# Turning a modulation group one step behind its products in a fused two-layer inference kernel

## The reference

```python
def adaln_params(cvec, w_mod, b_mod):              # once per layer, for c_ctx and for c
    m = jax.nn.silu(cvec) @ w_mod + b_mod          # (1024) @ (1024, 6 * 1024)
    ...                                            # -> sh1, sc1, g1, sh2, sc2, g2

def latent_layer(x, mods, ...):
    sh1, sc1, g1, sh2, sc2, g2 = mods
    h = rmsnorm(x, ln1_g) * (1 + sc1) + sh1
    (cb, cc, ch), (nq, nk, nv), (mq, mk, mv), mo, ig, fg = project(h, w_in, ml_gate_b)
    conv_o = cb * short_conv(cc * ch, conv_w)
    na_o = neighbourhood_attention(nq, nk, nv, k_ctx, v_ctx, na_rpb)
    ml_h, _, _, _ = mlstm_bidir(axial_rope(mq), axial_rope(mk), mv, ig, fg, C0, n0, m0)
    ml_o = mlstm_readout(ml_h, mo, ml_norm_g)
    x = x + g1 * merge(conv_o, na_o, ml_o, w_out)
    h2 = rmsnorm(x, ln2_g) * (1 + sc2) + sh2
    x = x + g2 * hier_moe(h2, ...)                 # 16 experts, top-2 in the top-1 group
    return x
```

## Time and profile before

| | us |
|---|---|
| median of 3 executions (1231.61 to 1316.1) | 1233.97 |
| the profiled execution, its own time | 1231.81 |
| its span | 1230.0 |
| PE busy in the span | 1145.1 |
| DVE busy | 409.4 |
| ACT busy | 250.2 |
| mean granted clock of PE, as a share of full speed | 0.975 |

### The profile page before, as it was taken

How to read it: one execution, slowest core, us unless ns; L and a number is a source line. 1 busy time by engine, 2 the same in 40 slices (tenths; PEclk the granted TensorE clock), 3 DMA queues, 4 the chain that set the end, 5 groups by cost and what they waited for, 6 DMA issues and landing times.

```text
span 1230.0 us, 15289 instructions
## 1 busy us (share of the span) xinstructions
PE 1145.1 (93%) x6240; PEld 623.2 (51%) x6240; DVE 409.4 (33%) x1150; ACT 250.2 (20%) x515; POOL 56.5 (5%) x82
## 2 busy tenths in 40 slices
PE   3999999898989999999989999998998999999996
PEld 3546555576544533554434564566654554355333
DVE  4402041355270333223252302224727032322234
ACT  2210121152132010110142011214413201011013
POOL 1230000000002000000020000000000000000001
PEclk8999999999999999999999999999998999999998
DMA  8967452277248989999971346234425698999991
GB/s 318 357 131 285 167 206 99 95 269 234 80 201 304 409 319 412 413 413 413 404 264 69 137 161 229 99 137 172 117 72 205 251 410 319 411 412 413 413 379 52
DMA packets 95512, 315.15 MB, mean 256 GB/s; under 512 B 5980, under 2 KB 6352, under 8 KB 86608
## 3 DMA queue, kind: packets, MB, share of 16 engines
q1 hardware_dynamic: 91856, 306.43, 65.1%
q0 software_dynamic: 3584, 7.71, 2.7%
HBM read 310.92 MB, written 4.99 MB: 257 GB/s over the span
## 4 chain that ended last, share of the span: by engine, by line
PE 85%; DVE 8%; ACT 3%; issue 2%; POOL 1%; DMA 1%; SPq 0%; DVEq 0%; POOLq 0%; ACTq 0%
PE ps L1341 18%; PE ps L944 16%; PE ps L1388 9%; PE ps L954 9%; PE ps L1112 6%; PE ps L1179 5%; PE ps L901 3%; PE ps L1207 2%; PE ps L891 2%; PE ps L1208 2%; PE ps L1231 1%; PE ps L1078 1%; PE ps L1143 1%; PE ps L934 1%; PE ps L1005 1%
## 5 line engine op out<-in xcount | busy, mean ns | idle before, releaser
L944 PE MATMUL ps<-ring,hT 128*128 128x512 f32 (+1 forms) x480 | 194.9, 565 | 0.0
L1341 PE MATMUL ps<-ring,arena 128*64 128x512 f32 x576 | 175.4, 595 | 0.0
L2014 DVE SCALAR_TENSOR_TENSOR xT<-ps,modT,xT 128x128 f32<-128x128 f32 x320 | 109.3, 410 | 193.9 <-PE ps L1208 106.0
L1341 PE MATMUL ps<-slot,arena 128*64 128x512 f32 x368 | 147.4, 596 | 0.0
L944 PEld LDWEIGHTS ps<-ring,hT 128*128 128x128 f32 x480 | 90.5, 190 | 98.0 <-issue 94.7
L954 PE MATMUL ps<-hT,ring 128*128 128x384 f32 x320 | 106.2, 489 | 0.0
L1388 PE MATMUL ps<-ring,arena 128*64 128x512 f32 x336 | 88.5, 613 | 8.1 <-ACT arena L1673 8.1
L1341 PEld LDWEIGHTS ps<-ring,arena 128*64 128x64 f32 x576 | 52.2, 137 | 78.9 <-issue 78.9
L1112 PE MATMUL ps<-mixT,ring 128*128 128x384 f32 x256 | 83.4, 487 | 1.7 <-ACT mixT L1601 1.7
L2238 DVE SCALAR_TENSOR_TENSOR y_low<-ps,route,y_high 128x512 fp32r<-128x512 f32 x32 | 23.9, 751 | 173.3 <-ACT y_high L1679 172.6
L954 PEld LDWEIGHTS ps<-hT,ring 128*128 128x128 f32 x320 | 59.8, 190 | 40.7 <-issue 0.8
(11 more groups left out here) (332 smaller groups left out, 1294.5 us busy)
## 6 DMA issues: line engine op xcount, KB each, us to landing
ring<-in_w_mod SPq DMA_DIRECT2D x24, 2048.0 KB, 11.7
ring<-in_w_down SPq DMA_DIRECT2D x44, 1024.0 KB, 13.7
ring<-in_w_up SPq DMA_DIRECT2D x40, 1024.0 KB, 11.3
ring<-in_w_gate SPq DMA_DIRECT2D x32, 1024.0 KB, 12.8
slot<-in_w_gate SPq DMA_DIRECT2D x30, 1024.0 KB, 13.1
ring<-in_w_in SPq DMA_DIRECT2D x14, 2048.0 KB, 12.3
slot<-in_w_up SPq DMA_DIRECT2D x22, 1024.0 KB, 10.3
slot<-in_w_down SPq DMA_DIRECT2D x22, 1024.0 KB, 11.3
```

The source lines that it names most:

```text
L944: mm = pe.matmul(p[:, 0:n], hT[:, k, t * P:(t + 1) * P], w[:, k, c0:c0 + n], start=(k == 0), stop=(k == KT - 1))
L1341: mm = pe.matmul(out[which][64 * s:64 * s + 64, :], xg[:, k, cols[s]], w[i][:, k % 4, :], start=(k == 0), stop=(k == KT - 1))
L2014: ins = dve.scalar_tensor_tensor(xT[:, m, cols], p[:, cols], modT[:, L, gate0 + m, j:j + 1], xT[:, m, cols], ALU.mult, ALU.add)
```

## The change

Turning a group becomes a step of its own, `("mod_turn", which, c)`, put into the list two places behind the fourth block of its group, so that exactly one other step stands between the two. The `modrow` copy stays in the step of the block. The part on PE (wait for the copy, four transposes) and the rest on DVE (`modT`, `gains`) are in the new step. The group ahead of layer 0's list is turned right behind its fourth block, as before. The second edit moves the four blocks of layer 1's first group in layer 0's matrix memory from ahead of reads 1, 3, 5 and 7 to ahead of reads 0, 2, 4 and 6. Nothing is computed differently, and the counts of instructions are the same.

```diff
@@ mixing_steps
     for dh in range(8):
         steps += [("decay", dh + 1)] if dh < 7 else []
-        steps += mods[:1] if dh % 2 else []
+        steps += mods[:1] if dh % 2 == 0 else []
         steps += [("read", dh)]
-        if dh % 2:
+        if dh % 2 == 0:
             del mods[:1]
     assert not mods
+    for i in reversed([i for i, step in enumerate(steps) if step[0] == "mod" and step[2] % 4 == 3]):
+        steps.insert(i + 2, ("mod_turn", *steps[i][1:]))
     return steps
@@ PE
                     if c % 4 == 3:
                         done(mm, name)
-                        bk.wait_drained(pe, name)
-                        turned = ("modT", which, c // 4)
-                        p = begin(turned)
-                        for i in range(4):
-                            mm = pe.transpose(p[:, i * P:(i + 1) * P], modrow[:, i * P:(i + 1) * P], ident)
-                        done(mm, turned)
                     else:
                         mm.then_inc(ly.mod_read, 1)
+
+                def mod_turn(which, c):
+
+                    bk.wait_drained(pe, ("mod", which, c // 4))
+                    turned = ("modT", which, c // 4)
+                    p = begin(turned)
+                    for i in range(4):
+                        mm = pe.transpose(p[:, i * P:(i + 1) * P], modrow[:, i * P:(i + 1) * P], ident)
+                    done(mm, turned)
@@ DVE
                     q = c // 4
                     p = full_of(("mod", which, q))
                     drain(("mod", which, q), dve.tensor_copy(modrow[:], p[:, :]))
+
+                def mod_turn(which, c):
+
+                    q = c // 4
                     p = full_of(("modT", which, q))
                     drain(("modT", which, q), dve.tensor_tensor(
```

More of the change, by code:

```diff
@@ L1096, in _ @@
                         mod(0, c)
+                    mod_turn(0, 3)
                     pe.wait_ge(const_loaded, 32)
-                steps = {"gates": gates, "by_token": by_token, "by_feature": by_feature, "mod": mod,
+                steps = {"gates": gates, "by_token": by_token, "by_feature": by_feature, "mod": mod, "mod_turn": mod_turn,
                          "gate_columns": gate_columns, "old_keys": old_keys, "turn": turn,
@@ L1978, in _ @@
                 norm(0)
-                steps = {"gates": gates, "mod": mod, "rope": rope, "by_feature": by_feature,
+                steps = {"gates": gates, "mod": mod, "mod_turn": mod_turn, "rope": rope, "by_feature": by_feature,
                          "context_scores": context_scores, "scores": scores, "context_turn": context_turn,
```

## The result

The changed kernel takes 1222.63 us (median of 4 executions, 1221.42 to 1223.99); the kernel before takes 1233.8 (median of 4, one more than in the table of before). The execution of 1316.1 us fell in a slow state and is left out of the ratio of the two. That ratio is 0.9916, 95% interval 0.9896 to 0.9935, so 10.4 us are gained, between 8.0 and 12.8. The prediction was 1220.5, between 1215 and 1227. The profiled execution took 1221.42, its span fell from 1230.0 to 1219.6.

The account below looks back on a forecast made before the run. The bound was taken to be PE's work plus its short waits for DVE and ACT. A 2.0, B 4.5, C 1.85 and D 4.1, less 1.2 and 0.2, plus 0.6, gave 11.7 us: 1220.5, range 1215 to 1227.

Parts of the forecast that it names:

- A: Blocks (0,7) and (1,7): PE's later wait, at the keys' turn, ends 1.0 us earlier a layer, 2.0 in all.
- B: Blocks (0,11) and (1,11): PE's wait of 2.25 us becomes about 1.55; gain 2.4 and 2.1, together 4.5.
- C: Read 0 in layer 0's matrix memory: a ready block fills PE's 1.88 us wait for scores; gain 1.85.
- D: Turn of (1,3) in layer 0's memory: PE's 2.64 us wait and 1.45 of low clock go; gain 4.1.
- the heads: Normalised heads of layer 0: late next once the earlier waits go; 0.2 us allowed as loss.
- Rival 3: The order does nothing: gaps return at the next wait for DVE, only 1.85 us gained, 1230; chance 0.04.
- rival 2: DVE bounds the tail: layer 0's heads stay late, D is given back, gain 8.4 us, 1223.5; chance 0.1.
- the load rival: A block of layer 1's weights lands late and PE waits at (1,1); 1235 us at 36; chance 0.02.
- both half-clock stretches: Slow PE clock behind A in each layer: one of the two was expected to go, adding 0.6 us.
- B's clock: Half-clock stretch behind B's wait: expected to stay in one of the two layers, 1.2 us lost.
- the clock reshuffles: Half-clock stretches come or go along PE's work, some 3.3 us either way, 1217 or 1223.5; chance 0.2.
- the likeliest case: All places gain as replayed: 11.7 us, own range 1218 to 1223; chance 0.64.

Follow-up runs that it names:

- turn-only: Changed kernel with layer 1's first blocks back at odd steps and (1,3) turned right behind its block; 0.9970 of the kernel before.
- even-only: Kernel before with only the blocks moved to even steps, every turn still right behind its block; 0.9959 of the kernel before.
- second profile: The changed kernel, unaltered, profiled once more; 0.9922 of the kernel before, median 1221.8 us, span 1215.5 against 1219.6.
- place A only: Kernel before with only groups (0,7) and (1,7) turned one step later; 0.9987 of the kernel before.
- copy late: Changed kernel with DVE's copy to modrow moved from the block's step to the head of the turn's step; 1225.2 us, one execution.

## Why the prediction was right, and where it was not

*The replay.* At all five places the waits came as replayed: A's second wait ended 1.1 us earlier (1.0 said), B's was 1.63 (1.55), none at C, none at D, 0.24 at the heads (0.2). The turn-only and even-only kernels divide them as the steps did. Rival 3 (nothing gained but C) and rival 2 (the heads give D back) are out; the load rival too: from 36 us on PE waits for no load in any run.

*A was mis-sized.* 1.0 a layer became 2.1 and 2.3, as both half-clock stretches went, and the term for them was 0.6 in all. Its size was wrong too: what A gained over the 1.1 of the chain is 1.0 and 1.2 us, not 0.6. But that they went was luck: in the second profile the one in layer 0 is back, behind the smaller waits.

*B's clock.* I took 1.2 off for a stretch that would stay in one layer. None did, in any kernel in which B's turn is a step apart. Nor does a wait of 2.25 fix it: in the kernels with the even steps only and with place A only, layer 1's turn at B waits 2.25 as before, and the granted clock stays at 1.00 there.

*Layer 1's memory.* The sum had 0 and it lost 3.2, at a wait that did not change. The rival "the clock reshuffles" was right about the mechanism: in the ledger it is active beside the likeliest case, with +1.8 at A (4.4 less 2.0 and 0.6), -3.2 here and -1.3 elsewhere. Together with the +1.3 at B these nearly cancel. So the total came within 1.3 us of the forecast in part by luck, while the waits came by the replay.

The loss here does not look like chance, though. The wait of 1.8 to 1.9 us at read 0 stands in fourteen layers of these profiles. In seven of them the wait at B just ahead was 2.25, and none has a half-clock stretch behind read 0. In six the wait at B was 1.63 or 0.28, and all have one. In the last (copy late, 1.03) there is none. So shrinking the wait at B was followed by a stretch at read 0 in every kernel but one in which read 0 still waited, and the forecast should have asked where the clock falls next, as it asked what is late next. What ties the two together is open.

The Trainium skill's sentence on a free-running monitor ("TensorE: Matmul & The Clock Gate", Part 1) fits the two profiles of one kernel that differ by 4.1 us. The two equal profiles of the kernel before neither bear it out nor speak against it, as no row shows where the monitor stood.

*The median.* 1222.6 lies 2.1 over the forecast: 1.3 is the profiled execution (1221.42 for 1220.1), and 0.8 that the median is 1.2 over that execution where I had allowed 0.4.

## What to carry to other kernels

Replay both engines' timelines with the new order; a wait for another in-order engine is the time at which that engine reaches the instruction, so what matters is the work queued ahead of the copy, and how far apart the two steps are matters only as far as it changes that. Ask of each instruction in the late chain whether it needs the thing waited for: the mask and the convolution did not. Taking them out of the chain removed about as much waiting (2.5 and 5.6 us) as moving the turn and the blocks did (7.4 to 8.8), and each shortened the time. When a few waits of 1 to 3 us are at stake, compare the sum of waits and the clock separately, and trust several timed runs over one profile's span.

## What the runs showed of the hardware

Span times one less the mean granted clock was between 18 and 34 us in this kernel. It differed between orders of the same work by more than the change's own gain, and by almost 3 us between two profiles of one program.

In all twelve profiles the granted clock falls at the same four places, two behind each layer's memory (in the kernel before around 360, 427, 947 and 1015), and each stretch counts for 1.7 to 5.1 us of that sum. At other places the same wait was followed by full clock in one kernel and by half clock in another: 1.88 us at read 0, 2.64 at the turn of (1,3), 2.25 at B in layer 1. The length of the last wait alone doesn't tell which it will be; at read 0 the wait at B ahead of it went with it in thirteen of fourteen cases.
